# A hybrid decoder step on one core: attention projected first and interleaved with the rest of the projection

## The reference

```python
z = rms_norm(x, norm1) @ w_in                     # 1024 -> 2312 columns, in this order:
mq, mk, mv, mo, mi, mf, aq, ak, av = split(z)     # 256 256 512 512 4 4 512 128 128
m_out = mlstm_mix(mq, mk, mv, mo, mi, log_sigmoid(mf), state)       # 4 heads, dk 64, dv 128
# sliding window attention: 8 query heads, 2 kv heads, 64 wide, query blocks of 128
logits = q @ k.T * 64 ** -0.5 + rel_bias[bucket(distance)]          # 128 x 256 per block and head
probs = softmax(concat([logits, sink]))[..., :-1]
a_out = probs @ v
y = x + concat([m_out, a_out]) @ w_out
y = y + moe(rms_norm(y, norm2))                   # top 4 of 32 experts, clamped SwiGLU
y = rms_norm(y, final_norm)
```

## Time and profile before

| | |
|---|---|
| median of 3 runs | 1686.52 us (1685.93 to 1686.83) |
| the profiled execution, its own time | 1686.04 us |
| its span in the trace | 1684.0 us |
| PE busy | 1542.7 us, 92% |
| DVE busy | 1270.2 us, 75% |
| ACT busy | 1045.1 us, 62% |
| POOL busy | 171.8 us, 10% |
| mean granted TensorE clock | 0.917 of full |
| moved by DMA | 464 MB, 276 GB/s |

### The profile page before, as it was taken

The page is one execution under the profiler, slowest core; times in us unless marked ns, Lnnn a source line. Parts: engine busy times, 40 slices in busy tenths (PEclk is TensorE's granted clock), DMA queues, the critical chain, the costliest instruction groups (busy, mean ns, idle before and its releaser), DMA issues.

```text
span 1684.0 us, 21300 instructions
## 1 busy us (share of the span) xinstructions
PE 1542.7 (92%) x7091; PEld 1085.9 (64%) x7091; DVE 1270.2 (75%) x1256; ACT 1045.1 (62%) x950; POOL 171.8 (10%) x181
## 2 busy tenths in 40 slices
PE   2998977887949999999999999999999999999993
PEld 1998544554436767767676676767767677676762
DVE  5310354434348999998999999999998999998995
ACT  3331223333227777777787778777777787778775
POOL 1000001000150100001100001000001000001000
PEclk9999556557959999999999999999999999999997
DMA  7523122011048999999999999999999999999994
GB/s 244 125 92 112 34 30 68 1 35 51 27 175 304 360 365 379 367 367 369 357 372 374 373 369 363 370 362 376 371 368 370 353 373 375 373 368 359 371 356 172
DMA packets 170428, 464.24 MB, mean 276 GB/s; under 512 B 14196, under 2 KB 28152, under 8 KB 170120
## 3 DMA queue, kind: packets, MB, share of 16 engines
q1 hardware_dynamic: 149664, 423.72, 67.9%
q0 software_dynamic: 8880, 24.00, 6.1%
q10 hardware_dynamic: 11848, 16.09, 3.6%
HBM read 445.81 MB, written 23.58 MB: 279 GB/s over the span
## 4 chain that ended last, share of the span: by engine, by line
PE 65%; issue 12%; DVE 11%; ACT 5%; DMA 2%; DVEq 2%; ACTq 2%; POOLq 0%; POOL 0%; SPq 0%
PE ps L1433 61%; DVE ring_r L392 6%; PE ps L1436 4%; ACT ring_r L897 2%; DVEq L1402 1%; ACT reg_a L910 1%; DVE reg_b L1396 1%; DVE reg_b L1391 1%; DMA reg_p<-in_w_in 1%; DMA out_p_n<-reg_x 0%; POOLq L570 0%; DMA acc_rows<-reg_a,pass_tok 0%; DMA reg_x<-in_x_prompt 0%; DVE reg_w L1307 0%; ACT ring L958 0%
## 5 line engine op out<-in xcount | busy, mean ns | idle before, releaser
L1433 PE MATMUL ps<-ring_r,reg_z_r 128*96 128x512 f32 x4608 | 1099.7, 395 | 8.1 <-DVE reg_z_r L1361 7.1
L1433 PEld LDWEIGHTS ps<-ring_r,reg_z_r 128*96 128x96 f32 x4608 | 737.3, 162 | 323.0 <-DVE ring_r L392 11.4
L392 DVE TENSOR_TENSOR ring_r<-ring,ring_r 128x2048 fp32r<-128x2048 f32 x387 | 868.0, 2283 | 82.0 <-ACT ring_r L897 82.0
L897 ACT ACTIVATE ring_r<-ring 128x2048 fp32r<-128x2048 f32 x387 | 736.6, 1916 | 166.4 <-PE ps L1433 165.6
L592 POOL DMA_INDIRECT acc_rows<-reg_a,pass_tok x32 | 46.1, 1440 | 1029.9 <-issue 993.6
L1433 PE MATMUL ps<-reg_a_r,ring_r 128*128 128x260 f32 x576 | 106.5, 284 | 0.0
L916 ACT ACTIVATE reg_z_r<-ps 128x384 fp32r<-128x384 f32 x130 | 59.1, 480 | 65.9 <-PE ps L1436 65.9
L1433 PEld LDWEIGHTS ps<-reg_a_r,ring_r 128*128 128x128 f32 x576 | 89.6, 188 | 1.0 <-issue 0.9
L1433 PE MATMUL ps<-ring,reg_a 128*128 128x512 f32 (+1 forms) x160 | 83.3, 681 | 1.7 <-issue 0.9
L563 POOL DMA_INDIRECT reg_a<-xhat_rows,pass_tok x34 | 71.9, 2114 | 21.2 <-issue 21.2
L1361 DVE TENSOR_TENSOR reg_z_r<-ps,reg_z_r 128x384 fp32r<-128x384 f32 x130 | 65.7, 545 | 9.5 <-ACT reg_z_r L916 9.5
(11 more groups left out here) (284 smaller groups left out, 1069.2 us busy)
## 6 DMA issues: line engine op xcount, KB each, us to landing
ring<-in_w_gate SPq DMA_DIRECT2D x131, 1024.0 KB, 7.2
ring<-in_w_up SPq DMA_DIRECT2D x128, 1024.0 KB, 5.3
ring<-in_w_down SPq DMA_DIRECT2D x128, 1024.0 KB, 8.3
ring<-in_w_in SPq DMA_DIRECT2D x9, 1024.0 KB, 14.0
ring<-in_w_out SPq DMA_DIRECT2D x4, 1024.0 KB, 4.9
reg_x<-in_x_prompt SPq DMA_DIRECT2D x4, 512.0 KB, 4.8
reg_x<-in_x_prompt ACTq DMA_DIRECT2D x4, 512.0 KB, 4.0
xhat_rows<-reg_b ACTq DMA_DIRECT2D x4, 512.0 KB, 2.6
```

The source lines that it names most:

```text
L392: return eng.tensor_tensor(rest_r(k), w, rounded_r(k).bitcast(F32), ALU.subtract)
L897: act.activation(rounded_r(k), ring[:, slot_of(k), :], ACT.Copy).then_inc(hi_ready, 1)
L1433: return pe.matmul(out, lhsT, rhs, start=start, stop=stop, skip_group_check=True)
```

## The change

- The columns of `w_in` are projected in another order: attention's q, k and v first, then the mLSTM's v, k, q, output gate. The unit is now a half block (one half of the tokens, 256 or 264 columns, 24 matmuls) and the program walks 38 such steps, alternating between two PSUM banks.
- Attention runs in 16 pairs of heads. From step 15 on each step is followed by parts of three pairs: the scores of pair n, the transposes of pair n-1, the product with the values of pair n-2. DVE and ACT handle a pair with instructions of twice the width (the exponents stay one per head).
- The four prompt tiles and the sample tile have places of their own (in ring slots that are not used yet) and are loaded without waits; the norm's gain is applied to the rows; the rounding of the transposed tokens moves from DVE to ACT, and the remainder takes one or two instructions instead of four. The first two steps run after the second tile, before tiles 3 and 4 are transposed.
- `w_in` and `w_out` use 4 slots; an expert's piece is loaded only when all of them are used, after the output projection. The remainders of the tokens and `mixT` lie in the other 4 slots.
- The bias write, its read and the swapped keys are issued by ACT at steps 2, 10 and 12; the copies of the old cache go from the start to the end of the projection.
- POOL's masks wait for `mixs_ready` instead of `mixa_ready`.

The core of the diff, in the order SP, POOL, ACT, DVE, PE (the loops over the steps are those of the last three):

```diff
+STEPS = [(0, 0), (1, 0), (0, 1), (1, 1)] + [(j, half) for j in range(2, NZ + 1) for half in range(2)]
+FIRST_PAIR = 15
+PAIRS = NT * AH // 2
+TOK_STEPS = {14: 0, 23: 1, 24: 2, 26: 3, 27: 4, 28: 5, 30: 6, 31: 7}
...
-            for i in range(NTILE):
-                if i >= 2:
-                    sp.wait_ge(xT_psum, 2 * (i - 1))
-                    sp.wait_ge(rms_ready, i - 1)
-                sp.dma_start(xbuf[0:rows(i), i % 2, :], x_rows(i)).then_inc(x_in[i % 2], 16)
+            for i in range(2):
+                sp.dma_start(x_tile[i][0:rows(i), :], x_rows(i)).then_inc(x_in[i], 16)
+            load_first(0)
+            for i in range(2, NTILE):
+                sp.dma_start(x_tile[i][0:rows(i), :], x_rows(i)).then_inc(x_in[i], 16)
+            for k in range(1, N_FIRST):
+                load_first(k)
...
+            sp.wait_ge(pieces_used, N_FIRST)
             load_experts(0)
...
-            pool.wait_ge(mixa_ready, NT)
+            pool.wait_ge(mixs_ready, 1)
             pool.wait_ge(pk_out, 32)
...
+            for m, (j, half) in enumerate(STEPS):
+                if m == 2:
+                    act.wait_ge(rows_made, 1)
+                    act.dma_start(sc_bias.rearrange("h (q m) -> h q m", q=P),
+                                  bias_rows.unsqueeze(1).to_broadcast([AH, P, RLEN])).then_inc(bias_out, 16)
+                if m == 10:
+                    act.wait_ge(bias_out, 16)
+                    skew = bass.AP(sc_bias.tensor, P - 1, [[RLEN - 1, P], [P * RLEN, AH], [1, 2 * P]])
+                    act.dma_start(bias, skew).then_inc(bias_in, 16)
+                if m == 12:
+                    act.wait_ge(proj_ready, 12)
+                    act.dma_start(ak_swap[0:64, :], zT[64:128, ZAK, 0:T]).then_inc(aksw_in, 16)
+                    act.dma_start(ak_swap[64:128, :], zT[0:64, ZAK, 0:T]).then_inc(aksw_in, 16)
+                if m % 4 == 2 and m // 4 + 1 < N_IN:
+                    round_w_in(m // 4 + 1)
...
+                act.wait_ge(proj_psum, m + 1)
...
+                    last = act.activation(zT[:, b, cs], ps[m % 2][:, 0:w], f, scale=sc)
                 last.then_inc(proj_ready, 1)
+                if m in TOK_STEPS:
+                    token_major(TOK_STEPS[m])
+                n = m - FIRST_PAIR
+                if 0 <= n - 1 < PAIRS:
+                    evac_pT(n - 1)
+                if 0 <= n < PAIRS:
+                    exponents(n)
+            act.dma_start(o["s_k"][0, :, 0:WIN - 1], a["cache_k"][0, :, 1:WIN]).then_inc(out_done, 16)
+            act.dma_start(o["s_v"][0, :, 0:WIN - 1], a["cache_v"][0, :, 1:WIN]).then_inc(out_done, 16)
...
+            for m in range(FIRST_PAIR, FIRST_PAIR + PAIRS + 3):
+                n = m - FIRST_PAIR
+                if n < PAIRS:
+                    logits(n)
+                if n % 4 == 1 and n > 1:
+                    normalise(n // 4 - 1)
+                if n % 4 == 2 and n > 2:
+                    mix_attention(n // 4 - 1)
+                if m % 4 == 2 and m // 4 + 1 < N_IN:
+                    rest_of_w_in(m // 4 + 1)
...
+            for m in range(2, len(STEPS)):
+                steps(m)
...
+                n = m - FIRST_PAIR
+                if 0 <= n < PAIRS:
+                    att_scores(n)
+                if 0 <= n - 1 < PAIRS:
+                    att_pT(n - 1)
+                if 3 <= n < PAIRS + 3 and n % 4 == 2:
+                    att_oT(n // 4 - 1)
+                if 0 <= n - 2 < PAIRS:
+                    att_pv(n - 2)
+                if m in TOK_STEPS:
+                    token_major(TOK_STEPS[m])
...
-            units = NT * AH
-            att_scores(1)
-            att_scores(2)
-            for n in range(1, units + 1):
-                if n + 2 <= units:
-                    att_scores(n + 2)
-                att_pT(n)
-                if n % AH != 1:
-                    att_pv(n - 1)
-                if n % AH == 0:
-                    att_pv(n)
             pe.wait_ge(mixs_in, 16)
-            pe.wait_ge(pT_ready, units)
```

More of the change, by code:

```diff
@@ L203, in hybrid_step @@
         y_out = ring[:, 0:NTILE, D:2 * D]
[L205 to L207 removed]
         gates = sb("gates", [8, TT])
+        att = sb("att", [P, 24])
         ident = sb("ident", [P, P])
@@ L619, in _ @@
             act.dma_start(reg_w[16:20, 0:P], a["m_gain"][0].rearrange("(c p) -> c p", p=P)).then_inc(consts_in, 16)
-            act.dma_start(b_if, a["b_if"].rearrange("a n -> n a"), **slow).then_inc(consts_in, 16)
             act.dma_start(sink_bc, a["sinks"].to_broadcast([P, AH])).then_inc(consts_in, 16)
[L622 to L628, removed]
+            act.dma_start(relT, a["rel_bias"].rearrange("b h -> h b"), **slow).then_inc(relT_in, 16)
@@ L634, in _, with round_xT @@
[L634 to L640, removed]
+            def round_xT(i):
+                r = rows(i)
+                for q in range(2):
+                    act.wait_ge(xT_psum, 2 * i + q + 1)
+                    act.activation(xnT_hi[:, 4 * q:4 * q + 4, i * P:i * P + r],
+                                   ps[4 + 2 * (i % 2) + q][:, 0:4 * P].rearrange("p (c t) -> p c t", c=4)[:, :, 0:r],
+                                   ACT.Copy).then_inc(xT_hi, 1)
@@ L662, in _, with evac_pT @@
-            act.wait_ge(tab_init, 16)
[L663 to L666, removed]
+            def evac_pT(n):
+                i, c, lo = n // 4, n % 2, P if n < 4 else 0
+                act.wait_ge(pT_psum, n + 1)
+                if n >= 2:
+                    act.wait_ge(pv_psum, n - 1)
+                act.activation(probT[:, c, :, lo:], ps[4 + c][:, :].rearrange("p (x k) -> p x k", x=2)[:, :, lo:],
+                               ACT.Copy).then_inc(pT_ready, 1)
@@ new lines, in exponents @@
+            def exponents(n):
+                i, c, lo = n // 4, n % 2, P if n < 4 else 0
+                act.wait_ge(logit_ready, n + 1)
+                for x in range(2):
+                    h = head(n, x)
+                    last = act.activation(prob[:, c, x, lo:], prob[:, c, x, lo:], ACT.Exp,
+                                          bias=nmax[:, h:h + 1], accum_out=asum[i % 2][:, h:h + 1])
+                last.then_inc(prob_ready, 1)
+                if n % 4 == 3:
+                    act.wait_ge(sinkin_ready, i + 1)
+                    act.activation(asnk, asnk, ACT.Exp).then_inc(sinkexp_ready, 1)
```

487 lines of the change are left out of this document (246 added, 241 removed).

## The result

The changed kernel takes 1633.3 us (median of 4 runs, 1631.6 to 1633.6), the old one 1686.7 beside it: a ratio of 0.968, 95% interval 0.967 to 0.970. Forecast were 1633 us. The total agrees better than its parts do, as the experiments show.

What follows compares the result with a forecast made beforehand. PE was taken as the bound, dense in the projection and at half clock in attention. Terms -17 + 36 + 4 + 1 + 2 + 1 - 82.3 + 1 + 1 gave -53.3, so 1633 us by the median, range 1616 to 1664.

Steps and rivals of the forecast that it cites:

- Attention's PE work, +36: Projection: attention's 77.6 us of PE work moves in and about halves at full clock, adding 36 us (26.9 to 38.8).
- handshakes, +4: Interleaved steps: of the attention stage's 14 us with PE idle, 0 to 14 come along; 4 us taken.
- Token turns, +1: Projection: the two token-major turns that now lie inside it add 1 us.
- Do DVE and ACT keep up?: Interleaved steps: a step has 5.1 us; DVE's roughly 2.7 us and ACT's about 3 us for a pair both fit.
- A: Interleaved steps: the clock swings, half the time at 1.2 GHz, +48, 1681 us; chance 0.08.
- C: Interleaved steps: PE stays at 1.2 GHz throughout, dense parts too, +97, 1730 us, slower than before; chance 0.05.
- Start, -17: Before the first projected matmul: three load-chain links go and one block's steps run earlier, saving 17 us (7 to 20).
- the wait for the third tile: Start: a link of the load chain before the first projected matmul that goes, 5.1 us.
- The bias table, +2: Projection: the table's write lands near 51 us; ACT waiting at step 10 could stop PE, 0 to 10 us, 2 taken.
- Handover, +1: Handover to the mLSTM: ACT's two old-cache copies ahead of ten small transfers cost -1 to +4 us, 1 taken.
- The stage that goes, -82.3: Separate attention stage: it disappears, so PE starts the output projection at about 288.4 instead of 370.7 us, saving 82.3.
- Behind it, +1 and +1: From the output projection on: later POOL masks cost 1 us (0 to 2), later-read expert pieces 1 us (0 to 6).

Runs made afterwards that it cites:

- the doubling: Changed kernel with every PE instruction of the attention pairs issued twice: 1666.3 us, +33.0 against 1633.3.
- the maximum twice: Changed kernel with DVE taking the maximum of each pair's logits twice, with a drain: 1633.4 us against 1633.3.
- the kernel with the small bias table: Changed kernel with the bias table written for 32 partitions instead of 128 and read back in four parts: 1624.3 us, -9.0.
- the fastest version: Changed kernel with quarter bias table, cache copies at step 20, SP issuing ten small transfers, DVE's wait for them moved to its first write over their source: 1615.8 us.
- the last two kernels: Changed kernel with quarter bias table, early cache copies and SP-issued small transfers, 1617.4 us; the same with DVE's wait for those transfers moved later, 1615.8 us.

## Why the prediction was right, and where only its total was

- **Attention's PE work, +36, and handshakes, +4.** 38.7 us measured for both, 32.6 of it PE's own work (the doubling). Of the other 6.1, the trace of the changed kernel shows 4.7: twelve gaps of 0.33 us ahead of the transposes (4.0 in all) and one wait of 0.7. The mechanism held; PE's work was 3 us smaller and the handshakes 2 us larger. (Of the three figures that the forecast gives for one head's parts, the 0.98 is a row of weight loads; only the remark on a pass's tail uses it.)
- **Token turns, +1.** The two turns lie inside the projection in the kernel with the pairs behind it too, so the 38.7 don't hold them, and no run measured them.
- **Do DVE and ACT keep up?** Yes, with reserve: the maximum twice costs nothing. The argument that each part of a pair has a step of its own was the one that mattered: without it, +52.6.
- **The clock.** It held at 1.00 from 80 to 160 us; A and C did not come. The Trainium skill, "TensorE: Matmul & The Clock Gate", section "A second HAM failure mode: psum-queue depth-cycling", tells of a kernel that cycles through PSUM banks, idles briefly between groups of matmuls and swings between the two levels. In the changed kernel the trace does not show that: PSUM banks rotate, but from 66 to 184 us PE waits for another engine only once, for 0.7 us, and the twelve gaps of 0.33 us did not lower the clock. In the kernel with both parts of a pair in one step, where PE idles 2.1 us a step, it does agree: the clock swings between 0.50 and 1.00, 0.87 on average. A clock that stays low, rival C, is not in that section, though the forecast put C under it.
- **Start, -17.** Measured -20.0, by other parts than named. The first transposes came 2.8 us earlier (12.12 against 14.88), for which I had 4.1. The 7 us that I gave to "the wait for the third tile" and "the wait for the sample tile" were right in size (8 us) and wrong in cause: the order of the loads, four weight pieces ahead of these tiles. The first block gave 5.9 for 5.75. Some 3 us more are not assigned.
- **The bias table, +2.** This step failed in size: 8.3 in the projection, 9 in all. "20 us; issued at about 31 us it lands near 51" took the rate of a stretch of the trace of before for the transfer's own; 1.5 MB took 34.6 us, in all ten kernels that write the whole table within 0.2 us (the chains show 34.49 to 34.81), whether it was issued at 27.7 us or at 36.1. The range of 0 to 10 held it; the value was taken at the wrong end, and the price of the clock behind the wait was not in it. The sign that the forecast named for it, PE waiting for ACT near step 10 to 12, is the wait in the trace.
- **Handover, +1.** 3.8, inside the range, by the collision that was named, on ACT's issues.
- **What the sum lacked.** -20.0 + 38.7 + 8.3 make 27.0, without the token turns, and the projection ends only 24.6 later. So some 3 us less lie between the blocks. I had not costed the nine one-element transposes with which PE released its pieces (the old kernel's `pieces_used`). Eight of them stood between two blocks, and each put about 0.3 us there: where nothing else stands between, the next block starts 0.43 us after the last pass instead of 0.12.
- **The stage that goes, -82.3.** -82.5: `mix_s` is issued 2.6 us after `sc_mix`, and PE starts 9.2 us after it:

```profile
307.35 0.49 ACTq L881 DMA_DIRECT2D sc_mix<-reg_w  x1
...
309.98 0.35 ACTq L886 DMA_DIRECT2D reg_w<-sc_mix  x1
...
316.50 3.75 PE L1497 MATMUL ps<-ring 128*128 128x512 f32 x4 [0.86 <-issue]
```

- **Behind it, +1 and +1.** The first sum comes 1.5 us later against the output projection's start, and the last one 2.1 us later. From that last sum to the first expert product both kernels take 41.0 and 40.9 us, so the 4 MB that are read later cost nothing; the total of this part was right, its split was not.

The errors cancelled: the start and the list between the blocks were some 3 us each better, PE's work with its handshakes 1 us better, the bias 6 to 7 and the handover 3 worse. A total within 1 us was partly luck; the gain itself was not.

## What to carry to other kernels

Look for a stage in which PE is busy at half clock beside one in which it is dense. Here the same pairs took 71.2 us by themselves and added 38.7 between dense matmuls, at the full clock, but only with a dense part for each pair's way through the other engines; a single call put into the wrong step cost nearly all of the gain. When a tile comes late, look first at what stands ahead of it in its queue, and only then at the wait that released it. A transfer moved to an earlier place needs its own duration, not the rate of the stretch it stood in.

## What the runs showed of the hardware

- The bias write, 1.5 MB of 1.5 KB rows from 8 partitions, took 34.5 to 34.8 us wherever it started, about 45 GB/s; with weight loads the queues moved 319 GB/s (66 to 68 us) and more.
- An issue on ACT's queue behind two memory-to-memory copies of 0.5 MB took 2.26 and 2.62 us, in the kernel with the small bias table 5.08, and 0.59 and 0.79 without the copies ahead of it. ACT's work stood behind such an issue (its copy at 189.07 us 4.1 us idle):

```profile
181.36 5.08 ACTq L778 DMA_DIRECT2D sc_q<-reg_b  x1
```

- In the start the passes stand 0.21 us apart (half pace) while the column of the granted clock says 1.00 for the stretch (18 to 22 us in the fastest version, 11 and 12 matmuls in 2 us); there the spacing of the matmuls is the better witness:

```profile
18.00:20.00 2.00, 2.00 (x11) 1.71 (x10) 2.00 (x5) 1.96 (x3) 2.00 (x10) 1.00 1.10 347
20.00:22.00 2.00, 2.00 (x12) 1.22 (x10) 1.93 (x3) 1.97 (x4) 2.00 (x4) 1.00 1.10 349
```

- How long the half pace lasts in the start differs: of the last two kernels, which have the same program up to there, the first has none from 17.84 us on, and the second has it until about 23.6 us and again from 30.5 to 33.9, where the column shows it too. Their third steps start 2.1 us apart.
